# Entry of a streaming encoder kernel: one ordered weight queue, halo products apart, second supertile projected tile by tile

## The reference, cut to what matters

```python
n = rmsnorm(x) * norm1_g
z = n @ w_in                       # 1536 columns: a (pool, 512) | u (512) | v (512)
pool = (trailing_mean(a, w) - a) @ pool_w * pool_scale     # w = 2, 4, 8, 16 by group of 128
gmlp = gelu(u) * (masked_ws @ gelu(v) + b)                 # chunks of 128 tokens
x = x + concat(pool, gmlp) @ w_out
x = x + relu(rmsnorm(x) @ w_up)**2 @ w_down
y = rmsnorm(x) * normf_g
```

## Time and profile before

| | us |
|---|---|
| median of 3 runs | 1248.77 |
| lowest and highest | 1247.27, 1249.0 |
| the profiled execution | 1248.57 |
| its span on the slowest core (4) | 1247.0 |
| spans of the 8 cores | 1242.1 to 1247.0 |
| PE busy on core 4 | 1232.1 (99%) |
| WV in the chain that ended last | 1% |

### The profile page before, as it was taken

How to read it: one execution, slowest core, us unless ns; L and a number is a source line. 1 busy time by engine, 2 the same in 40 slices (tenths; PEclk the granted TensorE clock), 3 DMA queues, 4 the chain that set the end, 5 groups by cost and what they waited for, 6 DMA issues and landing times.

```text
span 1247.0 us, 19037 instructions; the slowest of 8 cores (1242.1 to 1247.0 us)
## 1 busy us (share of the span) xinstructions
PE 1232.1 (99%) x6777; PEld 651.3 (52%) x6777; DVE 502.7 (40%) x924; ACT 374.6 (30%) x722; POOL 97.1 (8%) x171
## 2 busy tenths in 40 slices
PE   8999999999999999999999999999999999999998
PEld 4455545545545554554555455455545545554554
DVE  5664434444533442543344254234415433450313
ACT  5353313125322330432233043223304322420422
POOL 5010000001010010100001010100101010000000
PEclk9999999999999999999999999999999999999999
DMA  8999967459449537745853874585378448547862
GB/s 175 176 221 222 242 161 199 112 142 322 157 131 257 203 127 227 240 169 157 257 195 130 225 253 169 152 248 195 135 227 260 169 143 244 156 145 228 253 203 85
DMA packets 90671, 240.48 MB, mean 193 GB/s; under 512 B 57665, under 2 KB 57729, under 8 KB 67794
## 3 DMA queue, kind: packets, MB, share of 16 engines
q1 hardware_dynamic: 78480, 189.74, 49.2%
q0 software_dynamic: 11920, 49.19, 17.0%
q10 hardware_dynamic: 178, 0.33, 0.1%
HBM read 214.40 MB, written 34.43 MB: 200 GB/s over the span
## 4 chain that ended last, share of the span: by engine, by line
PE 96%; DMA 2%; POOL 1%; DVE 0%; issue 0%; ACT 0%; SPq 0%; POOLq 0%; ACTq 0%; DVEq 0%
PE ps L705 30%; PE ps L764 28%; PE ps L589 9%; PE ps L432 8%; PE ps L667 7%; PE ps L687 7%; PE ps L457 5%; PE ps L786 2%; DMA WV<-w_v 1%; PE ps L537 1%; DMA X<-xall 1%; PE ps L352 1%; POOL RS L330 0%; POOL RS L324 0%; DVE HB L341 0%
## 5 line engine op out<-in xcount | busy, mean ns | idle before, releaser
L705 PE MATMUL ps<-H2T,RING 128*128 128x384 bf16 x2304 | 384.1, 327 | 0.5 <-DVE X L691 0.5
L764 PE MATMUL ps<-RING,ST 128*128 128x512 bf16 x1632 | 353.7, 380 | 0.0
L705 PEld LDWEIGHTS ps<-H2T,RING 128*128 128x128 bf16 x2304 | 223.8, 98 | 147.8 <-issue 0.9
L764 PEld LDWEIGHTS ps<-RING,ST 128*128 128x128 bf16 x1632 | 159.6, 98 | 191.8
L317 ACT ACTIVATE JUNK<-X 128x1024 bf16<-128x1024 f32 (+2 forms) x104 | 106.4, 1023 | 436.0 <-DVE X L771 290.1
L709 ACT ACTIVATE ST<-ps 128x384 bf16<-128x384 f32 x288 | 140.5, 489 | 208.5 <-PE ps L705 208.4
L711 DVE TENSOR_TENSOR ST<-ST 128x384 bf16<-128x384 bf16 x288 | 96.9, 357 | 193.7 <-ACT ST L709 193.4
L771 DVE TENSOR_TENSOR X<-ps,X 128x512 f32<-128x512 f32 x48 | 33.2, 692 | 222.3 <-PE ps L764 222.3
L432 PE MATMUL ps<-HT,WAU 128*128 128x384 bf16 (+1 forms) x640 | 106.7, 327 | 1.4 <-DMA WAU<-w_au 1.4
L432 PEld LDWEIGHTS ps<-HT,WAU 128*128 128x128 bf16 x640 | 62.3, 98 | 43.4 <-issue 2.4
L687 PE MATMUL ps<-RING,ST 128*128 128x512 bf16 x384 | 83.7, 379 | 0.1
(11 more groups left out here) (103 smaller groups left out, 732.9 us busy)
## 6 DMA issues: line engine op xcount, KB each, us to landing
RING<-scr SPq DMA_DIRECT2D x144, 1024.0 KB, 5.5
RING<-w_mlp POOLq DMA_DIRECT2D x16, 1024.0 KB, 16.6
scr<-RING SPq DMA_DIRECT2D x16, 1024.0 KB, 10.4
yall<-X POOLq DMA_DIRECT2D x27, 512.0 KB, 11.5
X<-xall POOLq DMA_DIRECT2D x24, 512.0 KB, 5.5
X<-xall SPq DMA_DIRECT2D x9, 512.0 KB, 7.7
yall<-X SPq DMA_DIRECT2D x5, 512.0 KB, 8.2
WOUT<-w_out POOLq DMA_DIRECT2D x2, 1024.0 KB, 26.7
```

Source lines behind the costliest of these rows:

```text
L705: i_ = e.matmul(bank(ub)[:, 0:TOK], lhsT=RING[s][:, k, (m % 4) * 128:(m % 4 + 1) * 128], rhs=H2T[:, k, :], start=(k == 0), stop=(k == 7))
L764: i_ = e.matmul(bank(n)[:, :], lhsT=ST[:, kg * 8 + kk, n * 128:(n + 1) * 128], rhs=RING[s][:, kk, :], start=(kg == 0 and kk == 0), stop=(k ...
```

## The change

All of it is in the entry, and in how two weights lie in memory.

- w_au is stored as 8 contiguous blocks and loaded one m at a time; w_v as two contiguous halves. `shared` splits a transposed tile's copy between DVE and ACT.
- x of supertile 1 goes from SP's queue to POOL's, set between the WAU blocks. The first WAU load is released by the first x tile.
- The halo's columns leave the products of supertile 0; `gen_WI_halo` makes them later, 32 matmuls of 16 columns in one bank.
- `gen_WI_au` takes a range of tiles; supertile 1 is projected by tiles as they come. The x and weight loads, the pooling and the products are written in a new order.
- `load_mid` is released by WV's first half.

```diff
-    w_au = din("w_au", [128, 8, 8, 128])
-    w_v = din("w_v", [128, 8, 512])
+    w_au = din("w_au", [8, 128, 8, 128])
+    w_v = din("w_v", [2, 128, 4, 512])
...
         load_x(0)
-        for n in range(NT):
-            load_x(1, [("X", 0, n)], n, n + 1)
...
-            gate = [("WAU", 4)]
+            gate = [("WV", 0)]
...
-        def load_wau(m0, m1, gate=()):
-            add("pool", lambda e: e.dma_start(out=WAU[:, m0:m1], in_=w_au[:, m0:m1]),
-                after=gate, writes=[("WAU", m) for m in range(m0, m1)], dma=f"wau{m0}")
+        def load_wau(m, gate=()):
+            add("pool", lambda e: e.dma_start(out=WAU[:, m], in_=w_au[m]), after=gate, writes=[("WAU", m)], dma=f"wau{m}")
...
+            if shared is not None:
+                for q, k0, rk in (("dve", 4, shared), ("act", 0, dst_res)):
...
-                add("pe", mm, reads=B.HTk + ([("HT", NT)] if h0 == 0 else []) + [("WAU", m)], writes=[("BANK", fb)])
+                add("pe", mm, reads=B.HTk[n0:n1] + [("HTd", i, n) for n in range(n0, n1)] + [("WAU", m)], writes=[("BANK", fb)])
...
+        def gen_WI_halo():
+            fb = next_front()
+
+            def mm(e):
+                for m in range(4):
+                    for k in range(8):
+                        i_ = e.matmul(bank(fb)[:, m * 16:m * 16 + 16], lhsT=WAU[:, m, k, :], rhs=HT[:, k, 0:16],
+                                      start=(k == 0), stop=(k == 7))
+                return i_
...
+        gen_N1_T(0, 0, 1)
+        gen_warm(4)
+        gen_N1_T(0, 1, 2)
+        gen_warm(4)
+        gen_N1_T(0, 2, 3, shared=True)
+        gen_warm(3)
+        first_sq(1, 0)
+        first_rs(1, 0)
+        first_apply(1, 0)
+        load_wau(5)
+        gen_L(1, "pool", 2, 3)
+        load_wau(6)
+        load_wau(7)
+        gen_WI_au(0, 0, 1)
...
+        gen_WI_au(0, 1, 3)
+        gen_N1_T(1, 0, 1, shared=True)
+        gen_WI_au(0, 3, 4)
+        first_sq(1, 1)
+        first_rs(1, 1)
+        first_apply(1, 1)
+        load_rest()
+        load_mid()
+        gen_WI_au(1, 0, 4, 0, 1)
+        norm_T((HBH, DTall), HT, ("HT", NT), 0, 16)
+        gen_WI_au(0, 4, 5)
+        gen_WI_halo()
+        gen_WI_au(0, 5, 6)
+        gen_WI_au(1, 4, 6, 0, 1)
+        gen_PL(0, 0, 3)
+        gen_N1_T(1, 1, 2)
+        first_sq(1, 2)
+        first_rs(1, 2)
+        first_apply(1, 2)
+        gen_WI_au(0, 6, 7)
+        gen_WI_au(1, 0, 6, 1, 2)
+        gen_WI_au(0, 7, 8)
+        gen_N1_T(1, 2, 3)
+        gen_WI_au(1, 6, 8, 0, 2)
+        gen_PL(0, 3, 4)
+        gen_WI_au(1, 0, 8, 2, 3)
+        gen_PL(1)
+        gen_foldw()
```

More of the change, by code:

```diff
@@ L262, in load_x, with gen_L @@
                     after=gate, writes=[("X", b, n)], dma=f"xld{b}sp_{n}")
-        def gen_L(i, q="pool"):
+        def gen_L(i, q="pool", n0=0, n1=NT):
             b = i % NXB
-            for n in range(NT):
+            for n in range(n0, n1):
                 t = i * NT + n
@@ L344, in norm_apply, with norm_T, trh @@
             return hb
-        def norm_T(hb, dstT, dst_res, ncol0, np_=128):
+        def norm_T(hb, dstT, dst_res, ncol0, np_=128, shared=None):
+            src, res = (HB[hb], [("HB", hb)]) if isinstance(hb, int) else hb
+            if shared is not None:
+                for q, k0, rk in (("dve", 4, shared), ("act", 0, dst_res)):
+                    fb = next_front()
+                    def trh(e, fb=fb, k0=k0):
+                        for k in range(4):
+                            i_ = e.transpose(out=bankbf(fb)[:, k * 128:k * 128 + 128],
+                                             in_=src[:, (k0 + k) * 128:(k0 + k + 1) * 128], identity=IDB[:])
+                        return i_
+                    add("pe", trh, reads=res + ["IDB"], writes=[("BANK", fb)])
+                    o = dstT[:, k0:k0 + 4, ncol0:ncol0 + 128]
+                    i4 = bankbf(fb)[:, 0:512].rearrange("p (k t) -> p k t", t=128)
+                    if q == "dve":
+                        add("dve", lambda e, o=o, i4=i4: e.tensor_copy(out=o, in_=i4), writes=[("BANK", fb), rk])
+                    else:
+                        add("act", lambda e, o=o, i4=i4: e.activation(out=o, in_=i4, func=AF.Copy), writes=[("BANK", fb), rk])
+                return
             fb = next_front()
-            src, res = (HB[hb], [("HB", hb)]) if isinstance(hb, int) else hb
             def tr(e):
@@ L446, in gen_WI_au @@
                                                                   func=AF.Gelu_apprx_tanh),
                         writes=[("BANK", fb), B.UTk(m - 4)])
+        def gen_WI_halo():
+            fb = next_front()
+            def mm(e):
[3 more added lines that the diff above has]
+                                      start=(k == 0), stop=(k == 7))
+                return i_
+            add("pe", mm, reads=[("HT", NT)] + [("WAU", m) for m in range(4)], writes=[("BANK", fb)])
+            add("act", lambda e: e.activation(out=A[:, :, 0:16], in_=bank(fb)[:, 0:64].rearrange("p (g t) -> p g t", t=16),
+                                              func=AF.Copy),
+                writes=[("BANK", fb)] + [("Ah", g) for g in range(4)])
@@ L486, in gen_PL @@
                                    reads=Aall, dma=f"o_sps{s}"))
-            for g in range(4):
+            for g in range(g0, g1):
                 src = B.A[:, g, :]
```

91 lines of the change are left out of this document (31 added, 60 removed).

## The result

The changed kernel is slower. It took 1253.32 and 1252.64 us, against a median of 1248.18 (four executions) of the kernel before on the same chip: a ratio of 1.0038, 95% interval 1.0021 to 1.0054. Executions in which the cores of a whole die ran at a lower clock, two here, are left out of every ratio and median of this text. I had forecast 1246.2, in a range of 1243.0 to 1250.0.

The account below looks back on a forecast made before the run. A core's span was taken as 1188.4 us plus fold(1)'s start, bound by WOUT's landing (57.1 - 2.5 + 1.2 = 55.8 on core 4, 55.95 on core 1): 56.0 + 1188.4 = 1244.4, with 1.57 and 0.20 added 1246.2 us, range 1243.0 to 1250.0.

Parts of the forecast that it names:

- the small loads: PWF, BB, G2B (1 MB), released by WV's first half: nothing for fold(1); BB needed near 50 us, about 3 us cover.
- My own sum of the stream: Weight loads up to WOUT: landing moves from 57.1 to 55.8 on core 4, from 56.65 to 55.95 on core 1.
- A rule that I had cited: DMAs from any engine share the same 16 engines and interleave, so the queue chosen saves issue time only.
- the gain of the gaps: DMA idle between 17 and 28 us counted as gone: 2.5 us on core 4, 1.9 on core 1.
- C: Slower rival: one GpSimd queue can't keep 16 engines full with 512 KB pieces; WOUT near 61, 1251.5 or 1253; chance 0.10.
- The pieces' +1.2 us: Weight stream: three loads of two m become six of one, costing +1.2 us, 0 to +2.5.
- my sign of being right: In the profile after, TensorE waits 1 to 3 us for WOUT at fold(1) on every core.
- TensorE: Start at 16.4, stretch of 24.3 us up to the v products, which begin at 40.7 against 44.94.
- The halo: Products of the halo's columns: 32 added matmuls of 16 columns cost 1.4 us, net +1.2.
- VectorE's chain: Pooling to the end of POOLW runs 27.3 to 49.7; gating and casts end at 57.5, hidden before 59.3.
- rival B: Stream runs faster, WOUT lands before 54.2 and VectorE's chain binds: near 1243.7; chance 0.20.
- rival A': TensorE waits up to 3.2 us at fold(1), the half clock follows and costs 1.7: 1247.9; chance 0.28.

Follow-up runs that it names:

- the G2B experiment: Changed kernel with PWF and BB released by WAU 4, VectorE's norms reordered as in the order mended, and G2B released by WOUT's first half: 1247.48 us, ratio 0.9993; repeated, 0.9991.
- the first experiment: Changed kernel with the three small loads (PWF, BB, G2B) released by WAU 4 again instead of WV's first half: 1247.29 us, ratio 0.9995 to the kernel before.
- the order mended: Changed kernel with small loads released by WAU 4, halo's norm after VectorE's H2T copy, tile (1,2)'s norm ahead of pooling group 2: 1247.56 us, ratio 0.9996.

## Why the prediction was wrong, point by point

**The step that failed is the small loads.** "BB is then needed by VectorE near 50 us; it has about 3 us of cover as long as WOUT is late." The first half is right: POOLW was done at 50.4 to 52.7 and the sum came next. The second half was never worked out. The easy estimate is a release near 35 us (WV's first half) and the latency of before (14.3 us for BB on core 4, from 26.3 to 40.6), 49.3 in sum, and no harm in it. But that latency is of a load issued while WV was being queued; at 35 both loads of WOUT stand ahead. My own sum of the stream had WOUT end at 55.8, and BB, the second of three loads that take turns with WOUT's two, comes with that end. The number was in the sum, one paragraph above. I used it for WOUT and not for BB. Measured, BB landed at 51.8 to 56.2 and the sum that needs it waited up to 4.37 us.

The cover was wrong too. I counted to the output products, where the gating is needed as data. It is needed earlier as a reader of PSUM banks: on core 5 before, TensorE's program came to fold(0) at 50.6 and nothing showed, since GT ran in time. A bank is a second, earlier due time that no wait of the trace before shows.

**A rule that I had cited for the wrong load.** The rows show BB arriving 0.2 to 1.5 us behind the GpSimd loads queued before it, on all eight cores. The Trainium skill (DMA: Bandwidth & Descriptors, Issuing engines are not separate DMA queues) says that DMAs of any issuing engine run on the same 16 engines and interleave. I had weighed it against the gain of the gaps. It bore on BB: being on SyncE's queue gave BB no way around. The trace agrees, and shows by what measure they interleave: 114 packets against 113 on core 0, and 0.80 MB against 0.22. The small load gets half of the packets and not half of the bytes.

**No rival had it.** C, the slower one, was a stream that starves. The stream did not starve (1.05 in 17 to 28 us). The slower rival should have been a load that the change releases later, with its reader.

**The stream: right on the two cores that I summed, in part by luck.** Gaps gone, as counted. WOUT forecast at 55.8 (core 4) and 55.95 (core 1): with the small loads in their old place it ended at 55.4 and 55.8. In the changed kernel it ended at 54.9 and 51.0, so "nothing for fold(1)" was wrong in that direction too. PWF and BB travelled beside WOUT, but G2B's 512 KB had moved behind it (landed at 62.5 and 61.7). With G2B alone late, in the G2B experiment, WOUT ended at 52.9 and 51.0 on these cores; that G2B is the whole reason is not shown. The pieces' +1.2 us did not show, so the full gap term did not either: 57.1 to 55.4 is 1.7 us where the gaps alone were to give 2.5, and over all eight cores WOUT's end moved from 55.4 to 54.8 in the mean. The wait of 1 to 3 us for WOUT at fold(1), my sign of being right, came on no core of the changed kernel, and on none of the first experiment, where fold(1) began at 54.4 to 56.1.

**TensorE: products right, waits missed.** I forecast the v products at 40.7; they came at 42.0 to 44.4. On core 0 it started at 16.27 (forecast 16.4), and 43.93 - 16.27 less waits of 0.26, 0.18, 1.54 and 1.07 is 24.6 us, where I had 24.3. The waits are 1.54 for VectorE's copy of half of H2T, which stands behind the halo's norm of 1.27 us, and 1.07 for tile (1,2)'s norm, which stands behind three pooling groups. Both can be read in the order of VectorE's list without a time. With the small loads early they cost nothing, because WV would have been waited for instead. In the changed kernel itself WV was there at 36.8 to 38.9, and no run removes the two waits alone.

**The halo: mis-sized, in my favour.** 32 products of 16 columns take 28.67 - 27.86 = 0.81 us, 0.025 each; I had 1.4, by the halo's transposes. The Trainium skill (TensorE: Matmul & The Clock Gate, Wait — 56ns, not 53.3ns?) states that start to start never drops below about 25 ns, however few the columns. The trace agrees, and that figure was nearer than the row I took.

**VectorE's chain: too early.** Forecast 27.3 to 49.7; on core 0 it ran from 29.2 to 52.0, 1.9 of the 2.3 us from its later start behind TensorE's waits. With BB in time (first experiment) it is the limit by 0.3 to 0.55 us, near my rival B's mechanism.

**The clock**: rival A' had a half clock behind a long wait; it came, behind another wait. Core 0's account against the first experiment: 64.58 - 56.68 = 7.9 us, of which 1.2 are there when v starts (43.93 against 42.69), 3.26 + 0.95 are the waits, less 0.55 that the other has, and 1.7 the slow v product; the remaining 1.3 lie in fold(1) and the gating products behind it, 2.80 us from 61.78 to 64.58, where core 3 of the G2B experiment, without a wait there, took 1.53.

So where did the expected 2.6 us go? The two limits that I saw, WV and WOUT, did move. With BB mended the time is 1247.3, by the ratio 0.6 less than before (the interval holds no change), not 2.6: on the slowest cores three chains (WOUT's end, VectorE's gating, TensorE's own program) now end within about a microsecond of each other, and the three attempts to shorten one gave the gain to the next. What remains open is why the stream of one or two cores ends 3 to 6 us behind that of the others (50.9 to 57.4 in one execution, and partly on other cores the next time): it begins with x tiles that land late (engines waited 7.1 and 7.0 us for them on cores 3 and 5 of the G2B experiment, 3.7 on core 1), and no run here tells what does that.

## What to carry to other kernels

When a change releases a load later, take its new landing from what is queued ahead of it at the new place, not from its old latency, and set it against every reader. Count in packets and turns, not in bytes: here the second small load on SyncE's queue landed with the second big load on GpSimd's, whether it had 256 or 512 KB, and the first with the first.

A step that reads PSUM has two due times: when its result is needed, and when its bank comes round again. Count the rotation of banks between a product and its reader before saying that the reader has cover.

## What the runs showed of the hardware

- A load of 256 KB on SyncE's queue (BB) took 11.1 us beside WV, and 21.0 with PWF ahead of it on its queue and both WOUT loads on GpSimd's; PWF, of the same size, took 12.6 there. In GpSimd's own queue, ahead of WV and WOUT, BB took 6.6.
- With both queues filled the engines moved as many packets of one as of the other: 114 and 113 on core 0, 120 and 120 on core 1, for 0.80 and 0.22 MB, and 0.85 and 0.24.
- Matmuls of 16 columns cost 0.025 us each when queued back to back, 128 columns 0.056 to 0.059 (1.88 us for 32).
- Half the clock came behind waits of 3.26, 2.12 and 2.29 us (each with 0.95 more) on cores 0, 4 and 6, and not behind 2.63 and 0.95 on core 2, nor behind 3.67 us at the v products of core 3 with the order mended. In the kernel before with the late release it came on core 6 behind 1.28 and 0.95. The length of the wait alone did not decide it.
